# Output projections in products of 512 columns, with a cast of the next weights put out behind each

## The reference, cut to what matters

```
out = merged @ w_out                      # (512,1024) @ (1024,1024)
x   = layer_norm(ALPHA * x + out, ln_g, ln_b)
```

```
mix = concatenate([o_a * silu(g_a), o_b * silu(g_b), o_c * silu(g_c), o_d * silu(g_d)])
x   = x + mix @ w_out                     # (512,1024) @ (1024,1024)
```

## Time and profile before

| | |
|---|---|
| runs (3) | 1509.38, 1511.02, 1514.30 us; median 1511.02 |
| the profiled execution | 1511.78 us, its span 1510.0 us, mean granted clock 0.982 |
| PE | 1417.6 us busy, 94% of the span, 8202 matmuls |
| PEld | 1102.2 us, 73% |
| DVE | 856.4 us, 57% |
| ACT | 729.1 us, 48% |
| POOL | 384.7 us, 25% |
| DMA | 135.76 MB, mean 90 GB/s |

### The profile page before, as it was taken

The page is one execution under the profiler, slowest core; times in us unless marked ns, Lnnn a source line. Parts: engine busy times, 40 slices in busy tenths (PEclk is TensorE's granted clock), DMA queues, the critical chain, the costliest instruction groups (busy, mean ns, idle before and its releaser), DMA issues.

```text
span 1510.0 us, 21577 instructions
## 1 busy us (share of the span) xinstructions
PE 1417.6 (94%) x8202; PEld 1102.2 (73%) x8202; DVE 856.4 (57%) x1553; ACT 729.1 (48%) x1557; POOL 384.7 (25%) x273
## 2 busy tenths in 40 slices
PE   7999999999989999999988889999789989999697
PEld 6767677778987677787778856677568856677476
DVE  3655436466662653455577665457665475558655
ACT  3555447555244554555554544435544544436443
POOL 2232132246132322223553211412002112321001
PEclk9999999999999999999989999999999999999999
DMA  6413451226242221112255523511223422521211
GB/s 226 112 30 88 109 137 32 62 69 217 98 154 57 58 84 57 56 46 63 79 205 167 126 57 71 119 57 60 78 64 93 126 59 44 115 66 61 84 56 57
DMA packets 195373, 135.76 MB, mean 90 GB/s; under 512 B 91590, under 2 KB 185414, under 8 KB 195270
## 3 DMA queue, kind: packets, MB, share of 16 engines
q1 hardware_dynamic: 191494, 120.22, 28.9%
q10 hardware_dynamic: 3776, 14.16, 2.5%
HBM read 122.03 MB, written 12.32 MB: 89 GB/s over the span
## 4 chain that ended last, share of the span: by engine, by line
PE 74%; DVE 13%; ACT 7%; issue 2%; DMA 2%; POOL 1%; SPq 1%; ACTq 0%; DVEq 0%; POOLq 0%
PE pb L1487 19%; PE pb L1489 17%; PE pb L1488 17%; PE pb L1570 6%; PE pb L1509 6%; PE pb L1548 4%; ACT prob L1626 2%; ACT tmp L1626 2%; DVE wl L1993 1%; ACT wh L1645 1%; DVE prob L2245 1%; DVE xl L2000 1%; DMA wr<-w_out 1%; PE pb L1520 1%; PE pb L1557 1%
## 5 line engine op out<-in xcount | busy, mean ns | idle before, releaser
L2386 POOL TENSOR_TENSOR wl<-wr,wh 128x512 fp32r<-128x512 f32 x178 | 255.2, 1434 | 874.5 <-ACT wh L1645 870.6
L1487 PE MATMUL pb<-xh,wl 128*128 128x512 f32 (+1 forms) x880 | 354.4, 403 | 11.6 <-DVE xl L2000 8.4
L1489 PE MATMUL pb<-xh,wh 128*128 128x512 f32 (+1 forms) x880 | 327.0, 372 | 0.0
L1488 PE MATMUL pb<-xl,wh 128*128 128x512 f32 (+1 forms) x880 | 326.7, 371 | 0.0
L1993 DVE TENSOR_TENSOR wl<-wr,wh 128x512 fp32r<-128x512 f32 x208 | 165.8, 798 | 165.7 <-ACT wh L1645 165.3
L1645 ACT CAST wh<-wr 128x512 fp32r<-128x512 f32 (+1 forms) x386 | 219.4, 604 | 38.8 <-PE pb L1489 26.3
L1487 PEld LDWEIGHTS pb<-xh,wl 128*128 128x128 f32 x880 | 168.9, 192 | 77.5 <-issue 43.1
L1489 PEld LDWEIGHTS pb<-xh,wh 128*128 128x128 f32 x880 | 168.5, 191 | 29.5
L1488 PEld LDWEIGHTS pb<-xl,wh 128*128 128x128 f32 x880 | 169.7, 193 | 21.7 <-issue 3.2
L1487 PE MATMUL pb<-wh,xl 128*128 128x256 f32 x448 | 133.6, 298 | 16.5 <-DVE wl L1993 7.9
L1626 ACT ACTIVATE prob<-prob,small 128x512 f32<-128x512 f32 (+3 forms) x128 | 76.2, 596 | 138.7 <-DVE small L2208 138.5
(11 more groups left out here) (197 smaller groups left out, 2456.4 us busy)
## 6 DMA issues: line engine op xcount, KB each, us to landing
wr<-w_in SPq DMA_DIRECT2D x39, 1024.0 KB, 5.2
wr<-w_out SPq DMA_DIRECT2D x14, 1024.0 KB, 5.3
wr<-w_in SPq DMA_DIRECT2D x48, 256.0 KB, 4.6
wr<-w_branch SPq DMA_DIRECT2D x48, 128.0 KB, 2.3
x<-prob SPq DMA_DIRECT2D x12, 512.0 KB, 3.3
wr<-w_out SPq DMA_DIRECT2D x48, 128.0 KB, 3.0
wr<-w_mem_kv SPq DMA_DIRECT2D x4, 1024.0 KB, 5.6
prob<-x ACTq DMA_DIRECT2D x2, 2048.0 KB, 11.0
```

What stands on the lines that cost most here:

```text
L1487: e.matmul(ps, ll, rh, start=start, stop=False)
L1488: e.matmul(ps, lh, rl, start=False, stop=False)
L1489: t = e.matmul(ps, lh, rh, start=False, stop=stop)
L2386: t = e.tensor_tensor(wl[:, j % 2, c0:c1], wr[:, j % 2, c0:c1], wh[:, j % 2, c0:c1].bitcast(F32), ALU.subtract)
```

## The change

- `w_out` of the first block is cut into pieces of 4 rows x 512 columns: `woa` is rows 0 to 3, `wob` rows 4 to 7. A piece has as many elements as before, and there are as many pieces. A chunk of a cast is now one row.
- A tile's product with `woa` leaves its bank open, and the product with `wob` goes on in it (`out_rows1`). In layer 0 all four tiles go through `woa` and then `wob` of column half 0; column half 1 is a pair, `woa` and `wob` tile by tile. There the casts of mkv0 are put out behind the last tile's `woa` product, ahead of `advance_late`. In layer 1 `out_half` takes two tiles through `woa` of both column halves and then `wob` of both, with four banks held.
- A `tick` stands behind each of these products; `advance_late` is called behind each product in the second half of layer 1, as before.
- `w_out` of the second block: `wo2l` and `wo2h`, 3 rows x 512 columns each. Three tiles are held after `wo2l`; tile 0 is finished with `wo2h`, its bank given to tile 3, whose `wo2l` product comes then, and then the others are finished. D's tail is run out ahead of the third tile of the first piece.
- `resid` and `acc` work on 512 columns, half as many times; the norm aggregates two statistics a tile instead of four.
- The signal of the memory's load is split in two, one for each load.

```diff
-        out += [("wo", 8, 256, l, 256 * m) for _ in range(1 + l) for m in range(4)]
+        out += [("wo" + rows, 4, 512, l, 512 * m) for m in range(2) for rows in "ab"] if not l else []
+        out += [("wo" + rows, 4, 512, l, 512 * m) for _ in range(2) for rows in "ab" for m in range(2)] if l else []
...
-        out += [("wo2a", 6, 256, l, 256 * m) for m in range(4)]
+        out += [("wo2" + rows, 3, 512, l, 512 * m) for m in range(2) for rows in "lh"]
...
+        def out_rows1(w, i, b=None):
+
+            return drain(gemm("tok", w, 0, 512, ("m", l), range(4, 8) if b else range(4), tile=i, b=b, start=not b,
+                              end=bool(b), stop=bool(b)))
+
+        def out_half(tiles, beside):
+
+            held = {}
+            for m in range(2):
+                w = wnext("woa")
+                for i in tiles:
+                    held[m, i] = out_rows1(w, i)
+                    tick()
+                    beside(None, i)
+                wdone(w)
+            for m in range(2):
+                w = wnext("wob")
+                for i in tiles:
+                    out_tile(m, i, out_rows1(w, i, held[m, i]))
+                    tick()
+                    beside(m, i)
+                wdone(w)
...
+            def chains(m, i):
+                advance_late(late)
+                if m == 1:
+                    run(features(2, i - 2))
+
+            out_half((0, 1), lambda m, i: None)
             late += [settle(i) for i in range(2)]
+            out_half((2, 3), chains)
             late += [settle(i) for i in (2, 3)]
...
+        w = wnext("woa")
+        held = [out_rows1(w, i) for i in range(4)]
+        wdone(w)
+        w = wnext("wob")
         for i in range(4):
+            out_tile(0, i, out_rows1(w, i, held[i]))
         wdone(w)
         mem_features(1)
-        pair = [wnext("wo") for _ in range(2)]
+        pair = [wnext("woa"), wnext("wob")]
         st["hold"] = True
         for i in range(4):
...
+            b = out_rows1(pair[0], i)
+            if i == 3:
+                wdone(pair[0])
+                st["hold"] = False
+                while due:
+                    tick()
+                st["hold"] = True
+            advance_late(late)
+            out_tile(1, i, out_rows1(pair[1], i, b))
+            advance_late(late)
...
     def out_partial(l, before, box):
+        for m in range(2):
+            w, held = wnext("wo2l"), {}
+            for i in range(3):
+                if i == 2 and m == 0:
+                    rest_of(before)
+                held[i] = yield from out_rows(l, w, i)
+                tick()
+                yield
+            w2 = wnext("wo2h")
+            st["hold"] = True
+            yield from out_sum(l, w2, m, 0, held[0])
+            yield
+            held[3] = yield from out_rows(l, w, 3)
+            wdone(w)
+            st["hold"] = False
+            tick()
+            yield
+            for i in (1, 2, 3)[:3 - 2 * m]:
+                yield from out_sum(l, w2, m, i, held[i])
+                tick()
+                yield
...
-                x = xres[:, i, 256 * m:256 * m + 256]
-                t = e.scalar_tensor_tensor(x, x, float(ALPHA), bank(b)[:, 0:256], ALU.mult, ALU.add)
+                x = xres[:, i, 512 * m:512 * m + 512]
+                t = e.scalar_tensor_tensor(x, x, float(ALPHA), bank(b), ALU.mult, ALU.add)
...
-                x = xacc[:, i, 256 * m:256 * m + 256]
-                t = e.tensor_tensor(x, x, bank(b)[:, 0:256], ALU.add)
+                x = xacc[:, i, 512 * m:512 * m + 512]
+                t = e.tensor_tensor(x, x, bank(b), ALU.add)
```

More of the change, by code:

```diff
@@ L371, in pieces @@
             over = k + 1 >= len(ks)
-            put("mm", ks=ks[k:k + 1], k0=ks[0], first=at["start"] and k == 0, last=end and over, stop=stop and over,
+            put("mm", ks=ks[k:k + 1], k0=ks[0], row=FIRST_ROW.get(WEIGHTS[at["j"]][0], 0), first=at["start"] and k == 0, last=end and over, stop=stop and over,
                 done=False, **at)
@@ L945, in plan @@
             break
-        w = wnext("wo")
-        held = [drain(gemm("tok", w, 0, 256, ("m", l), range(6), tile=i, end=False, stop=False)) for i in range(4)]
+        w = wnext("woa")
+        held = [out_rows1(w, i) for i in range(4)]
+        wdone(w)
+        w = wnext("wob")
         for i in range(4):
[L949 to L953, removed]
+            out_tile(0, i, out_rows1(w, i, held[i]))
         wdone(w)
         mem_features(1)
-        pair = [wnext("wo") for _ in range(2)]
+        pair = [wnext("woa"), wnext("wob")]
         st["hold"] = True
         for i in range(4):
[L959 to L968, removed]
+            b = out_rows1(pair[0], i)
[8 more added lines that the diff above has]
+            advance_late(late)
+            if i == 3:
+                wdone(pair[1])
             late.append(settle(i))
@@ L1057, in project, with out_rows, out_sum, out_left @@
         yield
-    def out_partial(l, before, box):
-        for m in range(4):
-            w = wnext("wo2a")
-            held = {}
-            if m == 0:
[L1064 to L1067, removed]
-                b = yield from gemm("tok", w, 0, 256, ("y2", l), range(4 if i in held else 0, 6), tile=i, b=held.get(i),
-                                    start=i not in held)
-                put("acc", l=l, m=m, i=i, b=b)
-                give(b)
-                yield
-            if m < 3:
-                wdone(w)
-        box["w"] = w
-    def out_left(l, w, i):
-        b = drain(gemm("tok", w, 0, 256, ("y2", l), range(6), tile=i))
-        put("acc", l=l, m=3, i=i, b=b)
-        give(b)
+    def out_rows(l, w, i, b=None):
+        return (yield from gemm("tok", w, 0, 512, ("y2", l), range(3, 6) if b else range(3), tile=i, b=b, start=not b,
+                                end=bool(b), stop=bool(b)))
+    def out_sum(l, w, m, i, b):
+        yield from out_rows(l, w, i, b)
+        put("acc", l=l, m=m, i=i, b=b)
+        give(b)
+        tick()
+    def out_partial(l, before, box):
+        for m in range(2):
[17 more added lines that the diff above has]
+                yield from out_sum(l, w2, m, i, held[i])
+                tick()
+                yield
+            if m == 0:
+                wdone(w2)
+        box["left"] = w2, held
+    def out_left(l, left, i):
+        w, held = left
+        drain(out_sum(l, w, 1, i, held[i]))
     for l in range(2):
```

65 lines of the change are left out of this document (25 added, 40 removed).

## The result

The changed kernel takes 1496.28 us (median of four runs, 1493.14 to 1498.07) against 1510.2 us in the same comparison: a ratio of 0.9906, 95% interval 0.9886 to 0.9926, so 13.9 us less (11.2 to 17.2). The forecast was 1490.5 us, a gain of 20.5 (20.7 as added up from the profile): right in sign and inside the range, with a third of the forecast gain missing. Its profiled execution took 1497.5 us with a span of 1495.7, 14.3 less than the span before.

A forecast was written before the change was run, and what follows sets the result against it. TensorE, busy 94% of the span, was taken as the bound, plus its idle and slow places. L0 8.1 + L1 8.0 + S0 and S1 4.6 = 20.7 us off 1511.8 gave 1491.1, said as 1490.5 us; 8-in-10 range 1482 to 1505.

The forecast's parts named there:

- Products: All four stages: 448 narrow triples become 224 wide ones, 0.04 us saved per narrow pair, 9.0 us in all (4.5 to 13).
- L0, the start: Start of the first block's output projection in layer 0: waits for merged rows 4 and 5 go, gain 2.4 us.
- L0, the end: End of layer 0's first-block output projection: earlier mkv0 casts remove a wait, 2.3 us, and the low clock around it, 1.7.
- L1: First block's output projection in layer 1: 2.5 + 2.0 + 3.5 = 8.0 us gained, ends 2.6 and 15.
- first product to the third weight: Start of layer 1's first-block output projection: third weight starts 4.2 us sooner, 1.7 with a half clock; 2.5 taken.
- to the sum behind the fourth weight: Layer 1's first-block output projection, the two weights after the start: 13.3 us become 10.9, gain 2.4, of which 2.0 taken.
- second half, to the next stage's first product: Layer 1's first-block output projection, VectorE's half: 34.5 us become 29.1 to 29.6; 3.5 us of the 4.9 taken.
- Rival (a): Waits only move, VectorE's casts pacing L0 and L1, banks S; columns and little else stay: 1502 us, chance 0.25.
- S0 and S1: Product fills beside the second block's last attention in its two layers: 1.9 + 1.8 - 1.4 = 2.3 us each, together 4.6.
- the bank handed over: S0 and S1: the fourth tile waits behind VectorE's 0.68 us add, some 1 us at two places a layer; 1.4 charged.
- (c): Rival, slower: bank handover in S0 and S1 costs a wait like 3.59 us at four places: 1515.5 us, chance 0.06.
- (d): Rival: casts stay put relative to products, lost load cover costs 8 us over eight weights of L1: 1510 us, chance 0.06.

## Why the prediction was right, and by how much it was off

**Products, 9.0 us: right in the rate.** 0.043 us a pair in the trace, for 0.04, and 9.4 us in the runs (6 to 13). By stage the traces keep 7.6 of it.

**L0, the start, 2.4: right.** The waits for merged rows are gone; the memory's transposes start 3.8 us sooner, of which 16 + 16 pairs of the first half are 1.3, so 2.5.

**L0, the end, 2.3 + 1.7: right where it was read, wrong in what is kept.** The wait at mkv0 is gone and the clock is full. But I summed the stage up at its own end and asked "what is late next" only for the second weight of the pair (0.9 charged, 1.1 measured). Next was VectorE, with the steps put off by the earlier casts. The timeline of the changed kernel, VectorE and PE:

```profile
416.64 0.64 DVE L2192 SCALAR_TENSOR_TENSOR prob<-prob,pb 128x512 f32<-128x512 f32 x1
...
417.92 1.27 DVE L2205 SCALAR_TENSOR_TENSOR prob<-prob,stats,setA 128x1024 f32<-128x1024 f32 x1
...
419.11 1.78 DVE L2027 TENSOR_TENSOR wl<-wr,wh 128x512 fp32r<-128x512 f32 x1
...
421.50 1.28 DVE L2209 SCALAR_TENSOR_TENSOR prob<-prob,stats,setA 128x1024 f32<-128x1024 f32 x1
...
422.85 1.86 PE L1483 MATMUL pb<-cst,prob 128*128 128x128 f32 x8 [1.94 <-DVE prob L2209]
```

The last tile's sum starts at 416.64, some 3.2 us after its product ended, because two casts and behind them the last steps of tile 1's norm, a pass of 1.28 us among them, stand ahead of it; from there VectorE is busy with hardly a gap until the normalised tile 2 releases PE. A new wait of 1.94 us and the clock behind it (0.66 between 423 and 428) take back 3.6 of the 7.7. Halving the passes recovered 1.5 of them; the rest was not taken apart.

**L1, 8.0: too much, and two of its three terms wrong in opposite directions.** At the first transposes behind it the gain is 6.9 to 9.3 us in six traces of the same L1 code (mean 8.3), at the first product of the next stage, where the forecast was read, 5.1 to 7.9 (mean 6.8), and a stage later 3.6 to 7.6 (mean 5.8). By the three terms:

| | before, us | after, us | gain in six traces | forecast |
|---|---|---|---|---|
| first product to the third weight | 19.3 | 15.3 | 3.9 to 5.3 | 2.5 |
| to the sum behind the fourth weight | 13.35 | 11.1 | 2.3 | 2.0 |
| second half, to the next stage's first product | 34.5 | 32.8 | -1.2 to 1.7, mean -0.1 | 3.5 |

The gains are against the first trace of the kernel before; its second has 18.8, 12.0 and 35.0 us. The foreseen wait at the second weight is there (1.82 us at 773.03, for 2.0 and 0.7), its half clock too, and the third weight starts 15.3 us after the first, for the 15.0 laid out by hand; what I had taken off for the half clock was too much. The second half is the step that failed. It was to be 29.1 to 29.6 us with 3.5 of waits left; it is 32.8 in this trace and 35.7 in the second, longer than before. PE's waits in it, for casts and then for xl, were 6.0 and 1.6 us before; now they are 5.0 and 1.8, in the second trace 6.6 and 1.8. So VectorE's casts still stand late behind its norm steps, and the 8 us at L1's end was luck in part: the start gave more than I took, the half that I called VectorE's nothing on average. The second trace's 6.6 us are above the 6 that I had set as the point of being wrong. The second half from the sum ahead of it to the next stage's first product, with its three waits for casts and VectorE's line ahead of the second:

```profile
791.68 0.69 DVE L2192 SCALAR_TENSOR_TENSOR prob<-prob,pb 128x512 f32<-128x512 f32 x1 [0.36 <-PE pb L1523]
...
796.48 4.62 DVE L2205 SCALAR_TENSOR_TENSOR prob<-prob,stats,setA 128x1024 f32<-128x1024 f32 x2
...
801.02 1.77 DVE L2027 TENSOR_TENSOR wl<-wr,wh 128x512 fp32r<-128x512 f32 x1
...
802.85 0.50 PE L1521 MATMUL pb<-wh,xl 128*128 128x512 f32 x1 [0.33 <-DVE wl L2027]
...
807.25 0.50 PE L1521 MATMUL pb<-wh,xl 128*128 128x512 f32 x1 [2.75 <-DVE wl L2027]
...
816.52 0.50 PE L1521 MATMUL pb<-wh,xl 128*128 128x512 f32 x1 [1.89 <-DVE wl L2027]
...
824.49 0.39 PE L1521 MATMUL pb<-xh,wl 128*128 128x256 f32 x1 [1.82 <-DVE xl L2034]
```

Rival (a), that the waits only move, is what happened to the missing third: true of L1's second half and of the stretches behind L0 and L1, not of the whole.

**S0 and S1, 4.6: right in sum (5.1), not layer by layer.** S0 gains 2.9 to 4.0 in six traces of its code (mean 3.5), S1 1.3 to 2.3 (mean 1.6), for 2.3 each. The wait for D's low part, 3.6 and 3.2 us, is gone, and the third bank is waited for instead, 3.7 us. The charge of 1.4 us a layer for the bank handed over is not seen anywhere: attention work stands between.

**Not in the sum.** Between 1184 and 1377 us the changed kernel's first trace loses 1.9 us and its second 0.6, over unchanged code, and at 620 us both gain 1.5. Rivals (c) and (d) are not borne out: no bank is waited for at four places, and half loads change nothing. What the changed kernel's first trace keeps adds up to the 14.6 us at the end of its span: 4.2 in L0, 1.5 at 620 us, 5.5 in L1, 3.0 in S0, 1.9 lost ahead of S1 and 2.3 in S1.

## What the runs showed of the chip

**One idle stretch, two prices.** Around 620 us PE stands still for 1.7 us in both kernels, in the same code. Before, then after:

```profile
620.00:630.00 10.00, 8.28 (x34) 5.65 (x33) 6.38 (x12) 5.36 (x10) 4.66 (x3) 0.87 0.33 105
```

```profile
616.00:626.00 10.00, 8.29 (x45) 5.72 (x45) 6.21 (x11) 5.36 (x10) 4.83 (x3) 1.00 0.35 107
```

The clock fell behind it in one and not in the other: 1.5 us. It repeats: the seven traces that reach this place 4.0 to 4.6 us earlier than before all gain the 1.5 us, and none of the seven others does, whether they reach it up to 1.2 us later, 1.9 to 2.0 us earlier or 5.6 to 5.8 us earlier. So a change far upstream moves the time by 1.5 us here without touching anything.

**The same code, the clock on either side of a wait.** The changed kernel's two traces differ by 2 us behind L1. Stretches of 5 us from 808, of the first and of the second:

```profile
808.00:813.00 5.00, 5.00 (x16) 3.92 (x16) 3.63 (x7) 2.65 (x6) 2.57 (x2) 0.66 1.21 232
...
818.00:823.00 5.00, 4.67 (x29) 3.87 (x27) 4.59 (x8) 2.84 (x6) 1.73 (x1) 1.00 1.08 199
```

```profile
808.00:813.00 5.00, 5.00 (x23) 3.88 (x21) 3.52 (x7) 2.75 (x7) 2.58 (x2) 1.00 1.20 236
...
818.00:823.00 5.00, 5.00 (x17) 4.11 (x17) 3.65 (x6) 2.21 (x4) 0.00 (x0) 0.53 1.12 205
```

Both restart at 816.5 to 816.7, when VectorE's cast is done. In the first the half clock came ahead of that wait and only shortened it (1.89 us); in the second PE waited 3.52 us at full clock and was slow afterwards, on the path. So what one trace says of such a stage can be off by 2 us.

**VectorE beside GpSimd.** A normalisation pass takes 1.28 us alone, and the two at 796.48, beside GpSimd's casts, 4.62/2 = 2.31 each; a cast takes 0.69 and 1.77. The extra is 1.0 to 1.1 us. The half of it that the prediction argued with was a misreading of the merged line in the earlier trace rows: of those two passes the first took 1.61 us and the second 2.31, so the full extra was there before the change too. It is near what the rule of the Trainium skill (SBUF — State Buffer, SBUF: two separate sides) gives for a loser that waits out an instruction; a GpSimd cast takes 1.3 us here.

## What to carry to other kernels

Sum a stage's gain not at its own end but where the next engine has caught up: a wait that is removed by moving work ahead on an in-order engine puts off everything behind it there, and here 6 to 7 us of the 16 gained in the first block's two projections were given back within 20 to 84 us by unchanged code. And check a stage's terms one by one: L1's total came out near the forecast while the term for its second half was wrong. When products get shorter, count the places where side work is let go: leaving out the cast behind each product cost 31 us, more than twice the whole change. The fixed cost of a matmul is read from the starts of a steady stretch (0.043 us a pair here), and that term held best of all in its rate.
